# The last expert step of a mixture of experts: gate and up as two products with the depth halved over the array, a down product split around the turn, moments ahead of a branch

## The reference

```python
logits = (x @ w_router).astype(jnp.float32)
top_val, top_idx = lax.top_k(logits, TOP_K)          # TOP_K = 2
...
for e in range(N_EXPERTS):                            # 8 experts, D_FF_EXPERT = 3584
    h = jax.nn.silu(x @ w_gate[e]) * (x @ w_up[e])
    y = y + gate[..., e:e + 1] * (h @ w_down[e])
...
h = layer_norm(ALPHA * h + ff, ln_g[i, 2], ln_b[i, 2])
```

## Time and profile before

| | us |
|---|---|
| median of three runs | 2364.01 |
| the three runs | 2359.44, 2364.01, 2368.95 |
| the profiled execution | 2360.85 |
| its span | 2359.0 |
| TensorE busy in the span | 2260.9 (96%) |
| TensorE weight loads | 1331.0 (56%) |
| VectorE busy | 451.3 (19%) |
| ScalarE busy | 354.3 (15%) |

### The profile page before, as it was taken

The page is one execution under the profiler, slowest core; times in us unless marked ns, Lnnn a source line. Parts: engine busy times, 40 slices in busy tenths (PEclk is TensorE's granted clock), DMA queues, the critical chain, the costliest instruction groups (busy, mean ns, idle before and its releaser), DMA issues. The chain is left out here.

```text
span 2359.0 us, 31883 instructions
## 1 busy us (share of the span) xinstructions
PE 2260.9 (96%) x13831; PEld 1331.0 (56%) x13831; DVE 451.3 (19%) x1173; ACT 354.3 (15%) x891; POOL 108.0 (5%) x188
## 2 busy tenths in 40 slices
PE   8999999999999999999999998999899899989986
PEld 5769675687777567787758766333333233323322
DVE  3231002342000344200021534101010011101012
ACT  1330000161000123200001613110010011000000
POOL 2202000001000011000000200000000000000000
PEclk9799999999999999999998998999999999999998
DMA  9605424584444353444343434899999999999994
GB/s 305 216 17 205 166 85 163 149 196 165 150 143 138 100 199 141 152 160 143 104 149 134 149 116 160 341 368 406 407 405 409 404 409 404 409 400 409 400 409 183
DMA packets 196934, 564.32 MB, mean 239 GB/s; under 512 B 9832, under 2 KB 25384, under 8 KB 196792
## 3 DMA queue, kind: packets, MB, share of 16 engines
q1 hardware_dynamic: 187352, 536.95, 61.3%
q0 software_dynamic: 9440, 25.28, 3.7%
HBM read 554.60 MB, written 7.60 MB: 238 GB/s over the span
## 5 line engine op out<-in xcount | busy, mean ns | idle before, releaser
L1256 PE MATMUL ps_a<-hT,slots 128*128 128x256 f32 x864 | 190.9, 379 | 0.0
L1256 PE MATMUL ps_d<-hT,slots 128*128 128x256 f32 x864 | 190.9, 379 | 0.0
L1505 PE MATMUL ps_d<-slots,hT 128*32 128x512 f32 x1456 | 183.2, 593 | 6.9 <-DMA late<-in_moe_w_up 2.6
L1256 PEld LDWEIGHTS ps_a<-hT,slots 128*128 128x128 f32 x864 | 163.9, 190 | 27.3 <-issue 5.7
L1256 PEld LDWEIGHTS ps_d<-hT,slots 128*128 128x128 f32 x864 | 164.2, 190 | 22.3
L1505 PE MATMUL ps_d<-slots,N 128*32 128x512 f32 x1344 | 166.3, 593 | 8.1 <-DMA slots<-in_moe_w_up 3.0
L1054 PE MATMUL ps_a<-hT,slots 128*128 128x256 f32 (+1 forms) x768 | 144.3, 349 | 1.9 <-ACT hT L1791 1.5
L1054 PEld LDWEIGHTS ps_a<-hT,slots 128*128 128x128 f32 x768 | 127.4, 193 | 19.1 <-issue 5.6
L2767 DVE TENSOR_TENSOR proj<-proj,ps_d 128x512 f32<-128x512 f32 x33 | 22.7, 687 | 590.6 <-PE ps_d L1256 519.3
L2690 DVE TENSOR_TENSOR proj<-proj,ps_d 64x512 f32<-64x512 f32 (+2 forms) x32 | 22.1, 689 | 569.9 <-PE ps_d L1505 321.0
L1273 PE MATMUL ps_x<-slots,proj 128*128 128x512 f32 x264 | 121.6, 592 | 0.0
(11 more groups left out here) (403 smaller groups left out, 2587.7 us busy)
## 6 DMA issues: line engine op xcount, KB each, us to landing
slots<-in_moe_w_gate SPq DMA_DIRECT2D x43, 2048.0 KB, 20.6
slots<-in_moe_w_down SPq DMA_DIRECT2D x42, 2048.0 KB, 20.9
slots<-in_moe_w_up SPq DMA_DIRECT2D x41, 2048.0 KB, 23.0
slots<-in_ffn_w_gate_up SPq DMA_DIRECT2D x20, 2048.0 KB, 8.0
late<-in_moe_w_up SPq DMA_DIRECT2D x15, 2048.0 KB, 23.0
late<-in_moe_w_down SPq DMA_DIRECT2D x14, 2048.0 KB, 20.4
late<-in_moe_w_gate SPq DMA_DIRECT2D x13, 2048.0 KB, 23.9
slots<-in_ffn_w_down SPq DMA_DIRECT2D x10, 2048.0 KB, 8.1
```

The costliest lines, as they stand in the source:

```text
L1256: last = pe.matmul(b[:, f * S:(f + 1) * S], v[:, k, (f0 + f) * P:(f0 + f + 1) * P], hT[:, k, :], start=(k == 0), stop=(k == KD - 1))
L1505: last = pe.matmul(b[TILE * j:TILE * j + TILE, :], x[:, k, TILE * c:TILE * c + TILE], views[w][:, k % deep, 512 * h:512 * h + 512], start= ...
```

## The change

The last step gets an order of its own on three engines.

- TensorE (`last_step`): down 53; gate alone, then up alone (`by_halves`); down 54 for `f` 0 and 1; the turn; down 54 for `f` 2 and 3; then down 55 as before. `by_halves` gives the four column groups slots 0-31 and 32-63 over the first half of the depth and the same over the second half, so that rows 0-63 and 64-127 of its bank are two partial sums of the same thing.
- Gate: ScalarE copies the first partial sum to `gated`, VectorE adds the second, ScalarE writes SiLU of the sum twice, to rows 0-63 and 64-127. VectorE multiplies all 128 rows by both partial sums of up. The turn is now four matmuls with `folded`, the identity's left half plus its right half, which turns and adds the two partial products at once, into 64 columns each. `folded` is made once by VectorE at the start of the stage. ScalarE copies the turned 128 x 256 values to `hid_b`.
- Outcome of the last expert: VectorE copies the left half, ScalarE the right half; the scatter's first matmul waits for VectorE alone, and the second for ScalarE.
- `bn_stats` of each half of a tile follows its sum in `gather_out`, and `bn_aggr` its tile's second; `last_norm` has only the rest. The branch that is not taken gets its own moments.

The core of the diff (left out: the banks' bookkeeping, `folded` among the names, the moments in the branch not taken):

```diff
+                def last_step(q, late):
+                    down(late[0])
+                    pe.wait_ge(*lane.of(("xg", steps[q]["m"])))
+                    by_halves(q, "gate")
+                    by_halves(q, "up")
+                    down_few(late[1], (0, 1))
+                    pe.wait_ge(*lane.of(("folded",)))
+                    pe.wait_ge(*lane.of(("hid_a", q)))
+                    b, n = bank(lane, "a")
+                    pe.wait_ge(*emptied(lane, "a", n))
+                    for f in range(4):
+                        last = pe.matmul(b[:, FEW * f:FEW * f + FEW], hidden[:, 0, f * P:(f + 1) * P], folded,
+                                         start=True, stop=True)
+                    last.then_inc(*lane.tick(a_full, ("full", "a", n), ("hid_read", q)))
+                    down_few(late[1], (2, 3))
...
+                def by_halves(q, w):
...
+                    for k in range(KD // 2):
+                        for j, (part, c) in enumerate(((0, 0), (0, 1), (1, 0), (1, 1))):
+                            at = KD // 2 * part + k
+                            last = pe.matmul(b[TILE * j:TILE * j + TILE, :], x[:, at, TILE * c:TILE * c + TILE], v[:, at, :],
+                                             start=(k == 0), stop=(k == KD // 2 - 1))
...
@@ ScalarE, first_slots
+                    if q == len(steps) - 1:
+                        act.activation(gated[64:P, 0, :], b[0:64, :], ACT.Copy).then_inc(*lane.tick(act_order, ("gate_part", q)))
+                        act.wait_ge(*lane.of(("gate_whole", q)))
+                        for low in (0, 64):
+                            act.activation(gated[low:low + 64, 1, :], gated[64:P, 0, :], ACT.Silu).then_inc(
+                                *lane.tick(act_order, ("gate_silu", q)))
+                        b, n = bank(lane, "a")
+                        act.wait_ge(*lane.of(("full", "a", n)))
+                        act.activation(hid_b[:, :, 0:FEW], b[:, 0:4 * FEW].rearrange("p (f s) -> p f s", f=4), ACT.Copy).then_inc(
+                            *lane.tick(a_free, ("free", "a", n), *[("hid_turned", i) for i in step["groups"]]))
...
+                act.activation(y_e[0:FEW, 512:1024], b[FEW:P, :], ACT.Copy).then_inc(
+                    *lane.tick(act_order, ("y_right", EXPERTS - 1)))
...
@@ VectorE, first_slots
+                        do(dve.tensor_tensor(gated[64:P, 0, :], gated[64:P, 0, :], b[64:P, :], ALU.add),
+                           ("free", "d", n), ("gate_whole", q), sem=d_free)
...
+                        post(dve.tensor_tensor(hidden[:, 0, :], gated[:, 1, :], b[:, :], ALU.mult), ("free", "d", n),
+                             ("hid_a", q), ("hid_b", q), *[("e_hidden", i) for i in steps[q]["groups"]], sem=d_free)
...
@@ VectorE, gather_out
+                        if m == EXPERTS - 1:
+                            do(dve.tensor_tensor(y, y, b[:, :], ALU.add), ("free", "s", n), sem=s_free)
+                            half_moments(t, half)
+                            continue
...
@@ VectorE, last_norm
-                moments(0)
                 r = start_root(1, stat[:, 33:34], 1.0, LN_EPS)
-                moments(1)
```

More of the change, by code:

```diff
@@ L613, in build @@
         earlier, every = QK[:, 0, 0, :], QK[:, 0, 1, :]
+        folded = QK[:, 1, 0, 0:FEW]
         silu = flat[:, 2048:3072].rearrange("p (b s) -> p b s", b=2)
@@ L1483, in scatter @@
                     for half in range(2):
+                        if m == EXPERTS - 1 and t == 0 and half == 1:
+                            pe.wait_ge(*lane.of(("y_right", m)))
                         b, n = bank(lane, "s")
@@ L1568, in down_few @@
                     pe.wait_ge(*lane.of(("hid_turned", i)))
-                    for f in range(4):
+                    for f in fs:
                         for j, (c, half) in enumerate(((0, 0), (1, 0), (0, 1), (1, 1))):
                             o = TILE * c + (2 * TILE if at % 2 or at == per - 1 else 0)
-                            last = pe.matmul(b[TILE * j:TILE * j + TILE, :], hid_a[:, f, o:o + TILE],
+                            mine = hid_b[:, f, TILE * c:TILE * c + TILE] if i == len(downs) - 1 else hid_a[:, f, o:o + TILE]
+                            last = pe.matmul(b[TILE * j:TILE * j + TILE, :], mine,
@@ L1573, in down_few @@
                                              v[:, f, 512 * half:512 * half + 512], start=(at == 0 and f == 0),
                                              stop=(at == per - 1 and f == 3))
-                    down_end(i, last, n)
+                    if 3 in fs:
+                        down_end(i, last, n)
+                def by_halves(q, w):
+                    x = xs[side(steps[q]["m"]) % 2][:, :, columns_of(steps[q]["m"])]
+                    v = slot(steps[q][w][0])
+                    b, n = bank(lane, "d")
+                    pe.wait_ge(*emptied(lane, "d", n))
+                    for k in range(KD // 2):
[3 more added lines that the diff above has]
+                                             start=(k == 0), stop=(k == KD // 2 - 1))
+                    last.then_inc(*lane.tick(d_full, ("full", "d", n), ("used", steps[q][w][0])))
@@ L1605, in first_slots @@
                     if q == len(steps) - 1:
-                        for i in late:
-                            down(i)
-                        late = []
+                        last_step(q, late)
+                        continue
                     pe.wait_ge(*lane.of(("xg", m)))
@@ L1990, in first_slots @@
                             *lane.tick(a_free, ("free", "a", n), *[("hid_turned", i) for i in step["groups"]]))
-                outcome(EXPERTS - 1)
+                b, n = bank(lane, "x")
+                act.wait_ge(*lane.of(("given", EXPERTS - 2)))
+                act.wait_ge(*lane.of(("full", "x", n)))
+                act.activation(y_e[0:FEW, 512:1024], b[FEW:P, :], ACT.Copy).then_inc(
+                    *lane.tick(act_order, ("y_right", EXPERTS - 1)))
                 for _ in range(4):
@@ L2844, in _ @@
                                 expert(groups, first, e)
+                        dve.wait_ge(*lane.own())
+                        for t in range(T):
+                            for half in range(2):
+                                half_moments(t, half)
                     with dve.Else():
```

22 lines of the change are left out of this document (21 added, 1 removed).

## The result

The changed kernel took 2356.13 us in the median of seven runs, against 2363.64 for seven of the kernel before: a ratio of 0.9966, 95% interval 0.9952 to 0.998. A second comparison, twelve runs of the changed kernel against 23, gave 0.9984, interval 0.9968 to 0.9999; its two medians are 2357.93 and 2363.33 us. The forecast was 5.0 us less, 0.9979, and no change by the bound of 0.5%.

The account below looks back on a forecast made before the run. The expert stage was taken to be bound by its weights' DMA, leaving only the tail after the last weights. Gains of 3.7 + 0.73 + 0.54 = 5.0 us took 2363.3 to 2358.3 us, range 2352.5 to 2365.5.

Parts of the forecast that it names:

- the chances: Forecast 0.68, low clock as now 0.15, gate not early 0.06, slower 0.06, unlisted 0.05; measured same 0.93, faster 0.04, slower 0.03.
- What bounds the kernel: Expert stage runs at the pace of its weights' DMA; nothing ahead of the last blocks can move, only the tail after.
- Gate ahead of up: TensorE, last step: gate runs alone before up's weights land, 3.43 us each, so gate and up end 3.4 us sooner.
- SiLU hidden: ScalarE and VectorE, last gate: copy, sum and two SiLUs take 2.7 us while up runs, cover 2.0 us, cost nothing.
- The turn: TensorE between the halves of down 54: four real matmuls instead of transposes, 1.03 us plus 0.1, bounds 0.6 to 2.1.
- The clock: TensorE, down 55: runs at full clock, 3.43 + 0.2 instead of 5.34 us; 1.8 of the 3.7 us gain.
- the stretch that preceded the fall is gone: Reason given for full clock in down 55: the low-busy chain of SiLU, product, transposes and copy no longer precedes it.
- the rule on waits for DMA: Skill's warning that DMA waits between short matmul runs lower TensorE's clock; basis of the slower rival, 2369.7 us, chance 0.06.
- The outcome on two engines: Last expert's outcome copied by VectorE and ScalarE: first sum 1.91 us after the copy instead of 2.64, gain 0.73.
- Moments ahead of the branch: VectorE, end of kernel: 2.86 us paid before the branch, 3.40 saved behind it, gain 0.54.
- branch 1.05: VectorE, between the last sum and the moments: the time read from the profile before, in us.
- The sum: Gains 3.7 + 0.73 + 0.54 = 5.0 us, from 2363.3 to 2358.3 us; gain bounds 2.7 to 5.8.

Follow-up runs that it names:

- the split alone: Kernel before with only down 54 split in halves around the turn, gate and up still one round; from VectorE's product before the last step to span end 49.62 us, before 47.53 to 47.61.

## Why the prediction was right

The time, its sign and the chances held: 2356.13 us lies in the range of 2352.5 to 2365.5, and the change is within 0.5%. Step by step:

- **What bounds the kernel.** Right. No gain ahead of the tail stands out from the scatter between traces. That the scatter of the runs is larger than the change was said too; one cause of it, the clock's return between 100 and 130 us, only the runs showed.
- **Gate ahead of up.** Right: both products take 3.64 us with their drain (predicted 3.43 + 0.2), gate ends before up's weights land. Its worth is larger than the 3.4 of the sum when the split stays without it, 4.9 to 5.0 at the end of down 55, since the clock goes with it.
- **SiLU hidden.** Right, with a cover of 1.6 us instead of 2.0.
- **The turn.** Right: the first record at 2321.28, 0.11 behind the 4 rounds of down 54, and 1.04 us until the next product; predicted 0.1 and 1.03, from 496 records of the same shape.
- **The clock.** Right in size, 1.72 of 5.34 us, and in its being a matter of what stood ahead of down 55. But "the stretch that preceded the fall is gone" was only half the reason: a stretch of the same length with the new turn and less idle time in it doesn't tip it. And the term doesn't stand alone: where the clock was held without the rest of the change, the scatter gave it back. The wait for up, 0.67 to 1.50 us in seven traces with the new order and 1.07 to 1.17 in four with the old, never tipped it; one of 4.40 did. The prediction held the rule on waits for DMA against the wait of 1.17 us. But the Trainium skill (TensorE: Matmul & The Clock Gate, "HAM oscillation") describes runs of matmuls that are shorter than the wait behind them. Of the waits for up only the last is of that kind, 3.64 us of down 53 ahead of 4.40, and it agrees with the page.
- **The outcome on two engines.** Right to 0.01 us: 1.92 from copy to first sum. The traces show what no row of before did: two engines reading the two halves of one bank at once, each at its own pace, as the Trainium skill (PSUM — Partial Sum Buffer, "PSUM bank collisions") has it for different quadrants.
- **Moments ahead of the branch.** Wrong in sign. The sums with moments took 6.25 us (predicted 6.32), and 3.59 shrank to 0.19 as predicted. The term that failed is "branch 1.05", carried over unchanged. The 1.05 us were what showed of a branch that had begun under the last sum; behind an instruction that VectorE waits for, it is 2.07. The step costs 0.41 instead of gaining 0.54, and with moments behind the branch the 8.10 came back. The table load and the root were hidden as predicted, and by more: the load starts at 2337.04, 1.0 us ahead of VectorE's next step.
- **The sum.** 5.0 against 4.4 in the tail. The branch takes 1.0 off, up's earlier landing in that trace gives 0.5 back. That the two partly cancel is luck, and so is how near the time came: the first comparison's medians are 7.5 us apart and the second's 5.4, where the tail gained 4.4.

## What to carry to other kernels

A gap between two instructions on an in-order engine is not the price of what lies in it: look in the sequencer's own records at when that work began. If it began under the instruction ahead, then any wait put behind that instruction brings it into the open; registers that a branch needs are better loaded where the engine waits anyway. And hold a saving that comes from the clock against the next stretch that the same engine has: filling one gap moved the fall into the scatter. Work that had to be done anyway was no safeguard either, as the split alone shows; where TensorE came to the scatter at full clock, it kept it only where the idle time ahead of the scatter was short.

## What the runs showed of the hardware that was not expected

- VectorE's sequencer needs 0.55 us to load one token count into a register and 0.22 for the register work behind it, in both traces; ScalarE's needs less for the same, 0.47 and 0.17.
- Around 90 us TensorE waits and the clock falls to half. It was still at half between 110 and 120 us in thirteen traces, and back at full in one, which gained 7.5 us there. The 12.2 us between the first two spans say little about a change of 4.4.
- A stretch of 2.9 us between long runs of matmuls tipped the clock in three of three traces with four transposes in it, and in none of two with four real matmuls. The second kind also had 0.4 us less idle time in the stretch and a longer run ahead of it, so the traces don't single out the transposes.
- Idle time of 1.64 us ahead of the scatter, behind full-clock work, was followed by a fall in the scatter in two of two traces (scatter of 5.78 and 5.00 us instead of 3.85); 0.91 or 0.92 us was not, in nine.
